# Attention stage of a hybrid decoder: gate transposes moved behind the scores, keys rotated before queries, the key-value product split in two parts

## The reference

```
xn = rmsnorm(x, norm_w); z = xn @ w_in            # 1024 -> q 512 | k 128 | v 128 | gate 512 | u 512 | g 512
q, k = rope(rmsnorm(q, q_norm_w)), rope(rmsnorm(k, k_norm_w))        # per head of 64
s = q k^T / 8, masked to the last 128 keys, in 128-query blocks: each block sees itself and the block before
p = softmax([s, sink]) without the sink's column; a = (p v) * silu(gate)
y = state space model of u, GELU, half-GLU, * silu(g)
out = x + concat(rmsnorm(a), rmsnorm(y)) @ w_out
```

## Time and profile before

| | |
|---|---|
| median of 3 runs | 1777.87 us (1766.0 to 1778.02) |
| profiled execution, its own time | 1775.17 us |
| its span, first to last instruction | 1773.4 us |
| mean granted TensorE clock | 0.981 |
| busy in the span: PE, DVE, ACT, POOL | 95%, 67%, 35%, 20% |
| stretch of the attention stage | to about 730 us |

### The profile page before, as it was taken

How to read it: one execution, slowest core, us unless ns; L and a number is a source line. 1 busy time by engine, 2 the same in 40 slices (tenths; PEclk the granted TensorE clock), 3 DMA queues, 4 the chain that set the end, 5 groups by cost and what they waited for, 6 DMA issues and landing times. The chain is left out here.

```text
span 1773.4 us, 24711 instructions
## 1 busy us (share of the span) xinstructions
PE 1682.3 (95%) x8604; PEld 1350.6 (76%) x8604; DVE 1185.4 (67%) x2652; ACT 623.1 (35%) x1631; POOL 346.1 (20%) x425
## 2 busy tenths in 40 slices
PE   6899999999999999799999999787879999999999
PEld 5677777777777777588888888554657888888886
DVE  7787888767878887585634334799855656456532
ACT  5454455544455544422111111245442222222200
POOL 2122222212222221100014441022102111021110
PEclk9999999999999999899999999899989999999999
DMA  6311112213322110335536618476673545535222
GB/s 228 124 63 63 63 63 71 85 36 122 122 79 63 51 40 13 109 93 99 117 89 116 139 54 142 138 223 206 169 159 113 137 113 137 148 131 137 93 93 68
DMA packets 197420, 191.16 MB, mean 108 GB/s; under 512 B 118064, under 2 KB 153520, under 8 KB 197296
## 3 DMA queue, kind: packets, MB, share of 16 engines
q1 hardware_dynamic: 191360, 184.83, 37.9%
q10 hardware_dynamic: 5936, 4.75, 0.9%
HBM read 131.81 MB, written 57.73 MB: 107 GB/s over the span
## 5 line engine op out<-in xcount | busy, mean ns | idle before, releaser
L1165 PE MATMUL ps_b<-b_WH,b_XH 128*128 128x512 f32 (+1 forms) x776 | 286.2, 369 | 0.7 <-issue 0.4
L1167 PE MATMUL ps_b<-b_WH,b_XL 128*128 128x512 f32 (+1 forms) x776 | 276.9, 357 | 0.0
L1166 PE MATMUL ps_b<-b_WL,b_XH 128*128 128x512 f32 (+1 forms) x776 | 276.4, 356 | 0.0
L1165 PEld LDWEIGHTS ps_b<-b_WH,b_XH 128*128 128x128 f32 x776 | 148.1, 191 | 28.1 <-issue 8.8
L1167 PEld LDWEIGHTS ps_b<-b_WH,b_XL 128*128 128x128 f32 x776 | 147.8, 190 | 21.5
L1166 PEld LDWEIGHTS ps_b<-b_WL,b_XH 128*128 128x128 f32 x776 | 148.4, 191 | 18.6
L1120 POOL TENSOR_TENSOR b_XL<-b_XT,b_XH 128x1024 fp32r<-128x1024 f32 x33 | 80.9, 2451 | 376.0 <-ACT b_XH L1364 315.1
L1430 ACT ACTIVATE b_SM<-ps_b,b_small 128x128 f32<-128x128 f32 x256 | 113.7, 453 | 111.3 <-DVE b_small L1613 108.6
L795 PE MATMUL ps_g<-w_X0H,w_nextH 128*128 128x464 f32 x320 | 122.3, 382 | 2.7 <-DVEq L847 2.7
L797 PE MATMUL ps_g<-w_X0H,w_nextL 128*128 128x464 f32 x320 | 120.1, 375 | 0.0
L796 PE MATMUL ps_g<-w_X0L,w_nextH 128*128 128x464 f32 x320 | 119.9, 375 | 0.0
(11 more groups left out here) (339 smaller groups left out, 3768.0 us busy)
## 6 DMA issues: line engine op xcount, KB each, us to landing
b_XT<-in_xb SPq DMA_DIRECT2D x33, 512.0 KB, 4.1
b_XR<-in_x SPq DMA_DIRECT2D x33, 512.0 KB, 4.7
w_XT<-in_xt SPq DMA_DIRECT2D x36, 464.0 KB, 4.4
l_X<-in_xr SPq DMA_DIRECT2D x32, 512.0 KB, 4.4
out_out<-l_OUT SPq DMA_DIRECT2D x32, 512.0 KB, 3.0
scr_gs<-e_TG SPq DMA_DIRECT2D x36, 232.0 KB, 2.0
scr_u<-w_ST SPq DMA_DIRECT2D x12, 696.0 KB, 13.8
g_U<-scr_u SPq DMA_DIRECT2D x64, 130.5 KB
```

The costliest lines, as they stand in the source:

```text
L1165: pe.matmul(bank[:, 0:c1 - c0], XH[b][:, k, :], WH[:, k, c0:c1], start=(k == 0), stop=False)
L1166: pe.matmul(bank[:, 0:c1 - c0], XH[b][:, k, :], WL[:, k, c0:c1], start=False, stop=False)
L1167: mm = pe.matmul(bank[:, 0:c1 - c0], XL[b][:, k, :], WH[:, k, c0:c1], start=False, stop=(k == KD - 1))
```

## The change

On TensorE: `gate_transposes(t)` stands behind `scores(t)` and `samples(t)` instead of at the end of the loop before. `project_kv` is taken in two parts: its first two k-steps (6 matmuls of 256 columns) stand in front of the scores, behind `k_transpose`, and the other six behind the gate transposes. `project_q(t+1)` comes after that and is itself cut: six k-steps in front of `prob_transposes(t)`, two behind. KTB moves from bank 1 to bank 7, so that the key and value product need not wait for the copy of the transposed keys; it waits for the copies of the keys and the values out of bank 1 instead. On ScalarE: `gates(t)` stands in front of `exps(t)`; behind it come `copy_k`, `values`, `sum_out`, `samples`, `high_x(t+2)`, and only then `copy_q` and `square_qk`. On VectorE: the keys are rotated behind `normalise`, the queries behind `split_probs`; `gate_attn` comes in front of `gate_of`. GpSimd's and SyncE's queues are not edited. The number of instructions of each kind is the same.

```diff
--- before.py
+++ after.py
@@ -924,13 +924,14 @@
 
         ps = ctx.enter_context(nc.psum_tensor("ps_b", [P, 8, 512], F32))
         ZQ, ZKV, ZG, TB = (ps[:, b, :] for b in range(4))
-        KTB, SUMB, OB = ps[:, 1, 256:384], ps[:, 2, 0:2], ps[:, 4, :]
+        KTB, SUMB, OB = ps[:, 7, 0:P], ps[:, 2, 0:2], ps[:, 4, :]
 
         def scores_of(g):
             return ps[:, 4 + 2 * g:6 + 2 * g, :].rearrange("p b (j s k) -> p (b j) s k", j=2, s=2)
 
         NSTG = 9
         LAST, BEHIND = NT - 1, 3
+        EARLY_KV, EARLY_Q = 2, 6
         WH, WL = (shared.at("W" + hl, 0, "b_W" + hl, [P, KD, W1], F32R) for hl in "HL")
         STG = [shared.ST[:, (QK + P) * i:(QK + P) * (i + 1)] for i in range(NSTG)]
         NW, SA, EPSX = shared.NW, shared.SA, shared.EPSX
@@ -1168,17 +1169,19 @@
                     if k == KD - 1:
                         mm.then_inc(full, 1)
 
-                def project_q(t):
-                    pe.wait_ge(x_lo, t + 1)
-                    if t:
+                def project_q(t, part=range(KD)):
+                    if t and 0 in part:
+                        pe.wait_ge(x_lo, t + 1)
                         pe.wait_ge(q_out, t)
                         pe.wait_ge(gT_out, t - 1)
-                    project(t, ZQ, 0, DA, q_full)
-
-                def project_kv(t):
-                    if t:
-                        pe.wait_ge(kT_out, t)
-                    project(t, ZKV, DA, DA + 2 * P, kv_full)
+                    project(t, ZQ, 0, DA, q_full, part)
+
+                def project_kv(t, part=range(KD)):
+                    if 0 in part:
+                        pe.wait_ge(x_lo, t + 1)
+                        pe.wait_ge(k_out, t)
+                        pe.wait_ge(v_out, t)
+                    project(t, ZKV, DA, DA + 2 * P, kv_full, part)
 
                 def project_gate(t, part=range(KD)):
                     if t:
@@ -1267,7 +1270,7 @@
                     mm.then_inc(pv_full, 1)
 
                 def q_transposes(t):
-                    rope.wait(pe, tile(t), 4)
+                    rope.wait(pe, tile(t))
                     pe.wait_ge(qT_out, t - 1)
                     if taken(t - 1):
                         pe.wait_ge(s_out, taken(t - 1))
@@ -1277,8 +1280,8 @@
 
                 def k_transpose(t):
                     chain.wait(pe, tile(t))
-                    pe.wait_ge(k_out, t + 1)
-                    pe.wait_ge(v_out, t + 1)
+                    if t:
+                        pe.wait_ge(kT_out, t)
                     pe.transpose(KTB, RK[:], ID[:]).then_inc(kT_full, 1)
 
                 def gate_transposes(t):
@@ -1316,37 +1319,35 @@
                 project_q(1)
                 pe.wait_ge(const_ld, 16 * 6)
                 project_gate(0)
-                for t in range(NT):
-                    more = t + 1 < NT
-                    if t:
-                        scores(t)
-                        samples(t)
-                    if t == LAST:
-                        project_gate(t, range(BEHIND, KD))
-                    if more and t:
-                        project_q(t + 1)
-                    if 2 <= t < LAST:
+                k_transpose(0)
+                project_kv(1)
+                project_gate(1)
+                q_transposes(1)
+                k_transpose(1)
+                project_kv(2, range(EARLY_KV))
+                for t in range(1, LAST):
+                    scores(t)
+                    samples(t)
+                    gate_transposes(t)
+                    project_kv(t + 1, range(EARLY_KV, KD))
+                    if t >= 2:
                         total(t - 1)
-                    if t == 0:
-                        k_transpose(0)
-                    if more:
-                        project_kv(t + 1)
-                    if t:
-                        prob_transposes(t)
-                    if t == LAST:
-                        gate_transposes(t)
-                        total(t - 1)
-                    if t + 1 == LAST:
-                        project_gate(t + 1, range(BEHIND))
-                    elif more:
-                        project_gate(t + 1)
-                    if t:
-                        values(t)
-                    if more:
-                        q_transposes(t + 1)
-                        k_transpose(t + 1)
-                        if t + 1 < LAST:
-                            gate_transposes(t + 1)
+                    project_q(t + 1, range(EARLY_Q))
+                    prob_transposes(t)
+                    project_q(t + 1, range(EARLY_Q, KD))
+                    project_gate(t + 1, range(BEHIND if t + 1 == LAST else KD))
+                    values(t)
+                    q_transposes(t + 1)
+                    k_transpose(t + 1)
+                    if t + 1 < LAST:
+                        project_kv(t + 2, range(EARLY_KV))
+                scores(LAST)
+                samples(LAST)
+                project_gate(LAST, range(BEHIND, KD))
+                prob_transposes(LAST)
+                gate_transposes(LAST)
+                total(LAST - 1)
+                values(LAST)
                 last_total()
 
             @block.scalar
@@ -1370,13 +1371,13 @@
 
                 def copy_q(t):
                     act.wait_ge(q_full, t + 1)
+                    act.activation(RAW[:, 0:DA], ZQ, ACT.Copy).then_inc(q_out, 1)
+
+                def copy_k(t):
+                    act.wait_ge(kv_full, t + 1)
                     if t:
                         rope.wait(act, prev(t), 7)
                         act.wait_ge(qk_sq, t)
-                    act.activation(RAW[:, 0:DA], ZQ, ACT.Copy).then_inc(q_out, 1)
-
-                def copy_k(t):
-                    act.wait_ge(kv_full, t + 1)
                     act.activation(RAW[:, DA:QK], ZKV[:, 0:P], ACT.Copy).then_inc(k_out, 1)
 
                 def square_qk(t):
@@ -1480,8 +1481,8 @@
                 square_x(0)
                 high_w(KD)
                 high_w(KD + 1)
+                copy_k(0)
                 copy_q(0)
-                copy_k(0)
                 square_qk(0)
                 for n in range(KD + 2, 2 * KD):
                     high_w(n)
@@ -1493,6 +1494,8 @@
                 for t in range(NT):
                     if t >= 2:
                         square_a(t - 1)
+                    if 1 <= t < LAST:
+                        gates(t)
                     if t:
                         exps(t)
                     if t == LAST:
@@ -1500,19 +1503,19 @@
                         gates(t)
                         shared.high(act, 0)
                         next_high_x(0)
-                    if t + 1 < NT:
-                        copy_q(t + 1)
                     if t == 0:
                         keys(0)
+                    if t + 1 < NT:
+                        copy_k(t + 1)
+                        values(t + 1)
                     if t >= 2:
                         sum_out(t - 1)
-                    if t + 1 < NT:
-                        copy_k(t + 1)
-                        square_qk(t + 1)
-                        values(t + 1)
                     samples(t)
                     if t + 2 < NT:
                         high_x(t + 2)
+                    if t + 1 < NT:
+                        copy_q(t + 1)
+                        square_qk(t + 1)
                     if t == 0:
                         square_x(3)
                         square_x(4)
@@ -1523,8 +1526,6 @@
                     if t + 1 < NT:
                         queries(t + 1)
                         keys(t + 1)
-                    if t + 1 < LAST:
-                        gates(t + 1)
                 next_high_x(1)
                 shared.high(act, 1)
                 shared.high(act, 2)
@@ -1561,11 +1562,11 @@
                     cos, sin = (bcast_mid(TAB[b][:, i, part, :], h.stop - h.start) for i in range(2))
                     if part == 0:
                         dve.wait_ge(q_out, t + 1)
-                        dve.wait_ge(tabs, 2 * t + 2)
                         if t >= 2:
                             dve.wait_ge(qT_full, t - 1)
                     else:
                         dve.wait_ge(k_out, t + 1)
+                        dve.wait_ge(tabs, 2 * t + 2)
                     rope.mark(dve.tensor_tensor(s[:, :, 0:32], z[:, :, 32:64], sin[:, :, 0:32], ALU.mult))
                     rope.mark(dve.tensor_tensor(s[:, :, 32:64], z[:, :, 0:32], sin[:, :, 32:64], ALU.mult))
                     rope.link(dve, tile(t), dve.tensor_tensor(r, z, cos, ALU.mult))
@@ -1680,8 +1681,8 @@
                 low_w(KD)
                 low_w(KD + 1)
                 x_rsqrt(0)
+                rotate(0, 1)
                 rotate(0, 0)
-                rotate(0, 1)
                 for n in range(KD + 2, 2 * KD):
                     low_w(n)
                 norm_qk(0)
@@ -1694,20 +1695,21 @@
                     if t == LAST:
                         gate_of(t)
                     if t + 1 < NT:
```

(7 more changed lines are left out.)

## The result

The change makes the kernel slower: 1805.9 us median against 1772.8 for the kernel before, measured beside it, ratio 1.0171, 95% interval 1.0144 to 1.0198. (One more run of the kernel before, 1767.8, brought its median down from the 1777.9 that the prediction started from.) The profiled execution has a span of 1802.4 us, 29.0 more than before.

What follows compares the result with a forecast made beforehand. TensorE bounded the kernel; after the change VectorE's stalled chain would. 20 tiles at 21.6, 8 at 23.4, tile 15 at 29.9 and 1.4 gave 650.5 (+36); with +5 clock, 1816, plus 2.7 to the median: 1818, range 1768 to 1840.

Steps and rivals of the forecast that it cites:

- the first rival: VectorE's keys' rotation: `low_x` does not block it; ordinary tile 20.15, behind `x_rsqrt` 21.6, total 1771 us; chance 0.18.
- The pace and the slack: Attention tiles: TensorE sets the pace, VectorE near; RK has 0.5 us slack before the key transpose, then comes at +20.65.
- The start of `low_x`: GpSimd's subtraction starts at +9.6 to +9.75 instead of +13.19, blocking the last keys' rotation operation for about 2.4 us.
- the case in which `low_x` comes before the third rotation operation: Keys' rotation on VectorE: `low_x` precedes the operation of +9.59, so both last operations wait, 0.5 us more a tile.
- Ordinary tile: Scores to scores: RK at +20.65 delays key transpose and next scores; 21.6 us instead of 20.47.
- Behind `x_rsqrt`: Every fourth tile: maxima start 1.8 us late on VectorE, now the chain; 23.4 us instead of 21.05.
- The stretch: Scores of tile 2 to those of tile 31: 650.5 us instead of 614.4, 36 more.
- Tile 15: The tile bound by TensorE's long row of sample matmuls: 29.9 us, gaining 0.6 at its end.
- The clock: TensorE's waits bring the granted clock down in 5 of 28 tiles, delaying the maxima: +5 us.
- The start: Before tile 2's scores: about 1 us for gate transposes, 2 for a stall, 1 regained; taken as 0.

Runs made afterwards that it cites:

- e4: The changed kernel with no early k-steps of the key and value product in front of the scores: 1808.0 us, ratio 1.0188 to the kernel before.
- e7: The kernel before with `x_rsqrt` cut into two halves and its statistics taken three tiles at a time: 1772.7 us, ratio 0.9975.
- e1: The changed kernel with one wait more: GpSimd's `low_x` starts only when VectorE has rotated the keys: 1771.2 us, ratio 0.998 to the kernel before.
- e2: The kernel before with only ScalarE's `high_x` moved early, directly behind `copy_q`: 1847.7 us, ratio 1.0407.

## Why the prediction was right

**The number.** Forecast 1818, measured 1805.9. The stated range, 1768 to 1840, also held the first rival, in which the kernel gets a little faster, so the number alone would say little. What bears the forecast out is the mechanism: the stalled operation, the time at which `low_x` starts, and the wait for RK, all of which it had named.

**The pace and the slack.** It took the 0.5 us between RK and the key transpose as what to watch. RK came at +20.65 by the sum and at +20.6 in tile 25; the wait at the key transpose was forecast as 1.5 and is 1.34.

**The start of `low_x`.** Forecast +9.6 to +9.75, measured +9.60, which is the early end. I had given 0.5 us more a tile to the case in which `low_x` comes before the third rotation operation. It was issued in the same hundredth (both at 600.90), and that operation still took 0.29. That it fell on this side is luck: in tile 1, where `low_x` starts 0.07 ahead of the third operation, it is the third that takes 2.48. The price of that side was put too high as well: tile 8 of e4, where it happens, is 0.33 longer than e4's tiles 20 and 24, which in the changed kernel differ from tile 8 by 0.03 at most.

**Ordinary tile**: 21.6 forecast, 21.61 measured. **Behind `x_rsqrt`**: 23.4 forecast, 23.22 measured; the maxima were 1.64 late, not 1.8.

**What was too large.** The stretch was forecast at 650.5 and is 645.93. 8 tiles behind an `x_rsqrt` came to 182.9 instead of 187.2, since tiles 4 and 12 have sample work on ScalarE that pushes `low_x` off the rotation; the 20 others to 431.7 instead of 433.4, where tiles 9 and 13 escape in the same way (in tile 9 `low_x` comes so late that it holds the first operation of the queries' rotation instead, for 1.47). Tile 15 took 31.3 instead of 29.9, with its copy of the gates and 10.2 us at the lower clock instead of 6.8. The longer stretch at the lower clock need not come from the change: e7, which has the old order, has it too and took 31.74 there, against 30.51 for the kernel before. I had read the effect of sample work on TensorE and VectorE and left out ScalarE's, though the margin that I called a few tenths made it decisive. Of the 13 us by which its sum is too large (its terms add up to 1819), 4.6 are this stretch, 5 the clock, 3.2 the part behind the stretch, and 1.0 the distance from the profiled execution to the median, which was 1.7 and not 2.7; the start took 0.6 the other way.

**The clock.** The 5 us for five falls of the clock were not there: in the profiled execution of the changed kernel the clock falls in none of these tiles but tile 15. e4 shows that the case was real, four tiles, as soon as the six matmuls between the key transpose and the scores are gone.

**Rival 1** was priced at 20.15 a tile, 21.6 behind `x_rsqrt` and 1771 in all. e1 behaves like that kernel: 20.15, 21.67 and 1771.2. The two tiles are what the sum says; that the total agrees is luck. The stretch took 611.55 where the sum had 607.2, since tile 15 and the sample work cost more than it counted, and e1 is 3.8 us faster than the kernel before measured beside it (1774.95), not 7. What kept the case without a slowdown from coming about was 0.3 us of ScalarE's queue: in tile 14 `low_x` starts at +9.84 and the last operation of the rotation takes 2.50, in tile 13 it starts at +10.03 and the operation takes 0.29. The prediction had put the border at +9.9.

**The start** was counted as zero; the scores of tile 2 start 0.62 later: those of tile 1 come 1.00 later, as two of its terms add up to, and tile 1 then gains 0.38 and not 1. The part from the scores of tile 31 on took 1079.8, 3.2 less than before. Apart from tile 31 its code is the same in all nine versions, in which it ranges from 1079.8 to 1083.9; no run tells whether the change has a share in it.

## What to carry to other kernels

Price a reordering also by what each moved instruction releases on an engine that is far from setting the pace. Here ScalarE's copy came 3.6 us sooner, GpSimd's subtraction with it, and its 2.4 us fell on VectorE's critical chain. When an engine's busy time grows without more instructions, look for one whose duration has changed and for the other engine's instruction that ends when it does. Starting off-path work later, behind one more wait, can be the repair.

## What the runs showed of the hardware that was not expected

The Trainium skill (SBUF — State Buffer, "Who interferes with whom") was in the prediction with whose turn it is: whoever comes first keeps the pair for its instruction. The runs add the borders. A rotation operation already running is left alone, and GpSimd's instruction, issued in the same hundredth, has the next turn. Its record is then longer, 2.54 us instead of 2.41 where it starts beside a split, which looks as if it waited itself; in tile 5 of e2, issued 0.2 into an operation of 512 columns, it is 2.72. The stall follows GpSimd's length: 2.37 under 1024 columns, 1.26 under 512. The small table products of GpSimd do it in little: in e2 the operation on 512 columns behind the stall takes 0.95, next to them, instead of 0.69.

In e2 the granted clock of the stretch is 0.96, and in e4 it fell in four tiles where the changed kernel, with about as much waiting, kept it: an ordinary tile of e4 has a wait of 0.67 us in front of the key transpose and one of 0.49 in front of the scores, one of the changed kernel a single wait of 1.34 in front of the key transpose and six matmuls behind it. Whether the missing matmuls or the place of the waits does it was not tried.
